# Queries scaled in their copies, negated row maxima, moved copies, and two more tiny matmuls at each feed-forward head

## The reference

```
h = h + 0.5 * swiglu(rms_norm(h), w_gate, w_up, w_down)      # four times, D_FF = 2816
s_own = einsum('bqhd,bkhd->bqhk', q, k); where(causal, s_own, -inf); softmax     # moba, q * 128**-0.5
logits = einsum('bqgrd,bkgd->bgrqk', q, k) * 64**-0.5; softmax                    # ab, heads 0 to 7
logits = einsum('bhqk'...) * 64**-0.5 + bias[rel]; softmax                        # ab, heads 8 to 15
logits = (q . k) * 96**-0.5; softmax                                              # mla, 16 heads
h = h + square(relu(rms_norm(h) @ w1)) @ w2                   # twice, D_FF_2 = 4096
```

## Time and profile before

| | |
|---|---|
| median of 3 runs | 1597.22 us (1592.72 to 1602.87) |
| profiled execution | 1598.15 us, span 1596.2 us |
| TensorE busy | 1527.6 us (96%) |
| DVE busy | 1020.2 us (64%) |
| ScalarE busy | 760.3 us (48%) |
| GpSimd busy | 413.0 us (26%) |
| mean granted TensorE clock | 0.982 of full speed |

### The profile page before, as it was taken

One profiled execution on the slowest core, in us unless ns is written; L12 is line 12 of the kernel. 1 busy time (PEld: TensorE's weight loads), 2 busy tenths in 40 slices (PEclk: granted clock), 3 DMA queues, 4 the chain that ended last, 5 costly groups with the idle time before them and its releaser, 6 DMA issues.

```text
span 1596.2 us, 31933 instructions
## 1 busy us (share of the span) xinstructions
PE 1527.6 (96%) x13406; PEld 1483.9 (93%) x13406; DVE 1020.2 (64%) x1010; ACT 760.3 (48%) x995; POOL 413.0 (26%) x376
## 2 busy tenths in 40 slices
PE   9999995999999999999799999989999988999997
PEld 7999985999999999999699999968999987799997
DVE  6777768575566655566576556566755576675555
ACT  6444542554445544366554444666434356543333
POOL 2999925010002000038320000773000033410000
PEclk9999996999999999999999999999999998999999
DMA  7555544445554555545245555442454541245552
GB/s 271 187 209 184 200 95 139 175 170 203 183 208 171 212 188 184 186 161 185 77 165 208 208 187 187 156 146 87 183 207 165 202 158 54 80 179 191 184 184 79
DMA packets 54822, 271.19 MB, mean 170 GB/s; under 512 B 17681, under 2 KB 22033, under 8 KB 23345
## 3 DMA queue, kind: packets, MB, share of 16 engines
q1 hardware_dynamic: 53648, 266.58, 46.8%
q0 software_dynamic: 1088, 3.38, 0.6%
HBM read 266.52 MB, written 3.42 MB: 169 GB/s over the span
## 4 chain that ended last, share of the span: by engine, by line
PE 80%; DVE 6%; POOL 4%; DMA 3%; ACT 3%; issue 2%; SPq 2%; DVEq 0%; POOLq 0%; ACTq 0%
PE ps L675 76%; DVE xlo L1658 2%; DVE wlo L1652 1%; DMA turned_y<-gs 1%; PE ps L1049 1%; POOL tsq L307 1%; DMA turned_u<-sq 1%; PE ps L1073 1%; PE ps L1061 1%; DVE h L1674 1%; ACT whi L1231 1%; DMA raw<-in_wstream 1%; ACT pm L1498 1%; SPq L417 1%; SPq L406 0%
## 5 line engine op out<-in xcount | busy, mean ns | idle before, releaser
L1652 DVE TENSOR_TENSOR wlo<-raw,whi 128x2048 fp32r<-128x2048 f32 x245 | 573.0, 2341 | 238.0 <-ACT whi L1231 237.8
L1231 ACT CAST whi<-raw 128x2048 fp32r<-128x2048 f32 x245 | 468.0, 1911 | 263.0 <-PE ps L675 250.2
L675 PE MATMUL ps<-xhi,whi 128*128 128x256 f32 x2048 | 574.8, 281 | 5.4 <-DVE xlo L1658 3.6
L675 PE MATMUL ps<-xlo,whi 128*128 128x256 f32 x2048 | 571.7, 279 | 0.0
L675 PE MATMUL ps<-xhi,wlo 128*128 128x256 f32 x2048 | 571.6, 279 | 0.0
L675 PEld LDWEIGHTS ps<-xhi,whi 128*128 128x128 f32 x2048 | 386.5, 189 | 9.3 <-DVE xlo L1658 3.2
L675 PEld LDWEIGHTS ps<-xhi,wlo 128*128 128x128 f32 x2048 | 389.6, 190 | 0.0
L675 PEld LDWEIGHTS ps<-xlo,whi 128*128 128x128 f32 x2048 | 386.2, 189 | 0.0
L675 PE MATMUL ps<-hhi,whi 128*128 128x256 f32 x1216 | 340.0, 280 | 1.9 <-DVE hlo L1732 1.9
L675 PE MATMUL ps<-hlo,whi 128*128 128x256 f32 x1216 | 339.9, 279 | 0.0
L675 PE MATMUL ps<-hhi,wlo 128*128 128x256 f32 x1216 | 339.8, 279 | 0.0
(11 more groups left out here) (259 smaller groups left out, 1887.8 us busy)
## 6 DMA issues: line engine op xcount, KB each, us to landing
raw<-in_wstream SPq DMA_DIRECT2D x245, 1024.0 KB, 4.8
raw<-in_wstream SPq DMA_DIRECT2D x4, 512.0 KB, 7.3
h<-in_xT SPq DMA_DIRECT2D x4, 256.0 KB, 5.5
turned_u<-sq SPq DMA_DIRECT2D x8, 128.0 KB, 4.3
uP<-turned_u SPq DMA_DIRECT2D x8, 128.0 KB, 2.9
turned_y<-gs SPq DMA_DIRECT2D x8, 128.0 KB, 2.5
sq<-turned_y SPq DMA_DIRECT2D x16, 64.0 KB, 2.3
biasA<-bias_rows POOLq DMA_DIRECT2D x5, 192.0 KB, 5.3
```

Of the source, the lines that this page charges most:

```text
L675: return pe.matmul(o, l, r, start=first, stop=last, skip_group_check=True)
L1231: act.copy(whi[:, slot, :], raw[:, slot, :]).then_inc(S("whi_ready"), 1)
L1652: dve.tensor_tensor(wlo[:, slot, :], raw[:, slot, :], whi[:, slot, :], ALU.subtract)\
```

## The change

Four edits. (1) The copies that bring the turned queries to `qT` multiply by the heads' scale; the scale disappears from the mask and bias additions, from the exponents and from the maxima. (2) The maximum is written negated straight to `nmx`, with no second instruction and no wait between; `mx` goes. (3) In ab the odd head's copy is made by DVE only where all heads 2p to 2p+5 have no bias, that is for pairs 0 and 1; pairs 2 and 3 move to ScalarE. mla has no bias and stays. (4) `proj` can put a `settle` between its two halves, on the half of the bank that is written next. In each ffn stage it does so in the head's second projection and in the second round's first; in each mlp stage in the second and third round's. ffn3's second `settle` goes.

```
-            def settle(bank):
-                mm(ps[0:32, bank, 0:64], zrow[0:1, 0:32], zrow[0:1, 0:64], True, True)
+            def settle(bank, c=0):
+                mm(ps[0:32, bank, c:c + 64], zrow[0:1, 0:32], zrow[0:1, 0:64], True, True)
...
                 for m in range(2 if stop_k is None else 1):
+                    if between and m == 1:
+                        settle(bank, T)
...
-                        proj(n, i, 4 + 2 * b, after_fp32=u == 0 and i is None)
+                        proj(n, i, 4 + 2 * b, after_fp32=u == 0 and i is None, between=u == 1 and i is None)
                         if u == 0 and i is None:
                             pe.wait_ge(S("root_ready"), roots_upto(k))
-                        proj(n + 1, i, 5 + 2 * b, after_fp32=st == "ffn3" and u == 0 and i is None)
+                        proj(n + 1, i, 5 + 2 * b, between=u == 0 and i is None)
...
-                        proj(n, i, 4 + (1 + u) % 3, after_fp32=u == 0 and i is None)
+                        proj(n, i, 4 + (1 + u) % 3, after_fp32=u == 0 and i is None, between=u > 0 and i is None)
...
+                        if kind == "q":
+                            turned_row = act.activation(dst, src, ACT.Copy, scale=HEADS[st][0]["scale"])
...
-                        act.activation(pm4[s % 4][:, t, :], src, ACT.Exp, scale=sc, bias=nmx[:, s % 4, t:t + 1],
+                        act.activation(pm4[s % 4][:, t, :], src, ACT.Exp, bias=nmx[:, s % 4, t:t + 1],
...
+        def odd_on_vector(hs, p):
+            return all(hd["bias"] is None for hd in hs[2 * p:2 * p + 6])
...
-                    if hs[2 * p + 1]["bias"] is not None:
+                    if not odd_on_vector(hs, p):
                         turned(2 * p + 1)
...
-                            dve.scalar_tensor_tensor(out=lg[b][:, t, 0:w], in0=ps[:, b, t * T:t * T + w],
-                                                     scalar=hd["scale"], in1=mask[:, t, 0:w], op0=ALU.mult, op1=ALU.add)\
+                            dve.tensor_tensor(lg[b][:, t, 0:w], ps[:, b, t * T:t * T + w], mask[:, t, 0:w], ALU.add)\
                                 .then_inc(S(st + "_lg"), 1)
...
-                            chain(dve.reduce_max(mx[:, b, t:t + 1], lg[b][:, t, 0:n_keys(hd, t)], AX.X))
-                        dve.tensor_scalar(nmx[:, b, :], mx[:, b, :], -1.0, None, ALU.mult).then_inc(S(st + "_nmx"), 1)
+                            reduced = dve.reduce_max(nmx[:, b, t:t + 1], lg[b][:, t, 0:n_keys(hd, t)], AX.X, negate=True)
+                        reduced.then_inc(S(st + "_nmx"), 1)
...
-                    chain(dve.reduce_max(mx[:, b, :], src, AX.X))
-                    dve.tensor_scalar(nmx[:, b, :], mx[:, b, :], -scale, None, ALU.mult).then_inc(S(st + "_nmx"), 1)
+                    dve.reduce_max(nmx[:, b, :], src, AX.X, negate=True).then_inc(S(st + "_nmx"), 1)
...
-                    if hs[2 * p + 1]["bias"] is None:
+                    if odd_on_vector(hs, p):
                         turned_odd(2 * p + 1)
```

More of the change, by code:

```diff
@@ L164, in build @@
         krp = sb("krp", [P, TT, 96])
-        mx = sb("mx", [P, 4, TT])
         nmx = sb("nmx", [P, 4, TT])
@@ L684, in chunk_ready, with proj @@
                 pe.wait_ge(S("wlo_ready"), at_iter(n + 1, BODY, i))
-            def settle(bank):
-                mm(ps[0:32, bank, 0:64], zrow[0:1, 0:32], zrow[0:1, 0:64], True, True)
-            def proj(n, i, bank, operand=None, wait_k=None, first_k=0, stop_k=None, after_fp32=False):
+            def settle(bank, c=0):
+                mm(ps[0:32, bank, c:c + 64], zrow[0:1, 0:32], zrow[0:1, 0:64], True, True)
+            def proj(n, i, bank, operand=None, wait_k=None, first_k=0, stop_k=None, after_fp32=False,
+                     between=False):
                 ohi, olo = operand or (xhi, xlo)
@@ L1428, in turned @@
                     if kind in "qk":
-                        dst = (qT if kind == "q" else kT)[:, i0:i0 + 2, :]
+                        dst, src = (qT if kind == "q" else kT)[:, i0:i0 + 2, :], bank2(bank)
                         if c["rev"]:
-                            act.copy(dst.rearrange("p m (t c) -> p (m t) c", t=TT), reversed_tiles(bank2(bank)))\
-                                .then_inc(S(st + "_rowT"), 1)
-                        else:
-                            act.copy(dst, bank2(bank)).then_inc(S(st + "_rowT"), 1)
+                            dst, src = dst.rearrange("p m (t c) -> p (m t) c", t=TT), reversed_tiles(src)
+                        if kind == "q":
+                            turned_row = act.activation(dst, src, ACT.Copy, scale=HEADS[st][0]["scale"])
+                        else:
+                            turned_row = act.copy(dst, src)
+                        turned_row.then_inc(S(st + "_rowT"), 1)
                     elif kind == "cq":
@@ L1494, in exponents @@
                         if hd["bias"] is None:
-                            src, sc = ps[:, SCORE_BANKS[s % 4], t * T:(t + 1) * T], hd["scale"]
+                            src = ps[:, SCORE_BANKS[s % 4], t * T:(t + 1) * T]
                         else:
-                            src, sc = lg[s % 2][:, t, :], 1.0
-                        act.activation(pm4[s % 4][:, t, :], src, ACT.Exp, scale=sc, bias=nmx[:, s % 4, t:t + 1],
+                            src = lg[s % 2][:, t, :]
+                        act.activation(pm4[s % 4][:, t, :], src, ACT.Exp, bias=nmx[:, s % 4, t:t + 1],
                                        accum_out=rs[:, s % 4, t:t + 1]).then_inc(S(st + "_exp"), 1)
@@ L1551, in turned_unit @@
                         act.wait_ge(S("mla_qt"), 2 * u + m + 1)
-                        act.copy(qT[0:96, 4 * u + 2 * m:4 * u + 2 * m + 2, :], bank2(4 + 2 * (u % 2) + m)[0:96])\
-                            .then_inc(S("mla_qTc"), 1)
+                        act.activation(qT[0:96, 4 * u + 2 * m:4 * u + 2 * m + 2, :], bank2(4 + 2 * (u % 2) + m)[0:96],
+                                       ACT.Copy, scale=HEADS["mla"][0]["scale"]).then_inc(S("mla_qTc"), 1)
                 queries(0)
@@ L1992, in maxima @@
                         dve.wait_ge(S(st + "_exp"), 2 * (s - 3))
-                    src, scale = bank2(bank), hd["scale"]
+                    src = bank2(bank)
                     if hd["bias"] is not None:
@@ L2001, in maxima @@
                         for t in range(TT):
-                            dve.scalar_tensor_tensor(out=lg[s % 2][:, t, :], in0=ps[:, bank, t * T:(t + 1) * T],
-                                                     scalar=scale, in1=row_[:, P - P * t:P - P * t + T],
-                                                     op0=ALU.mult, op1=ALU.add).then_inc(S(st + "_lg"), 1)
+                            dve.tensor_tensor(lg[s % 2][:, t, :], ps[:, bank, t * T:(t + 1) * T],
+                                              row_[:, P - P * t:P - P * t + T], ALU.add).then_inc(S(st + "_lg"), 1)
                         dve.wait_ge(S(st + "_lg"), 2 * hd["n_bias"] + 2)
-                        src, scale = lg[s % 2][:, :, :], 1.0
-                    chain(dve.reduce_max(mx[:, b, :], src, AX.X))
-                    dve.tensor_scalar(nmx[:, b, :], mx[:, b, :], -scale, None, ALU.mult).then_inc(S(st + "_nmx"), 1)
+                        src = lg[s % 2][:, :, :]
+                    dve.reduce_max(nmx[:, b, :], src, AX.X, negate=True).then_inc(S(st + "_nmx"), 1)
                 def turned_odd(s):
```

## The result

The changed kernel takes 1573.51 us (median of 4 runs, 1572.75 to 1575.22), the kernel before 1594.97 beside it (4 runs, 1592.22 to 1602.87): ratio 0.9859, 95% interval 0.9821 to 0.9897. That is 21.5 us less. The forecast was 1575 us, 22.4 less than the 1597.2 it started from.

A forecast was written before the change was run, and what follows sets the result against it. TensorE was taken as the bound, with 80% of the last-ending chain. From 1597.2 us, 14.7 (tiny matmuls, net) and 7.7 (attention) came off, giving 1574.8, forecast 1575 us; range 1566 to 1597.

The forecast's parts named there:

- What bounds the kernel: Whole kernel: 80% of the last-ending chain is TensorE; feed-forward streams keep 113.1 or 117.5 ns per matmul at clock 1.00.
- Cost of the tiny matmuls: Feed-forward heads: 11 more tiny matmuls at 0.33 us each, 3.6 us, nothing hiding it.
- Gain from the pace: ffn2, mlp0, mlp1: slow streams turn fast, 4.4 ns per following matmul, 18.3 us; 14.7 net.
- Two independent tries: Feed-forward heads: two tiny matmuls, from 3 fast of 6 outcomes, turn a slow stage fast with 0.75.
- Rival 1: Feed-forward streams: pace doesn't depend on the tiny matmuls, or slow stays slow; 1593.1 us; chance 0.23.
- Rival 2: Feed-forward streams: only one or two of the three slow stages convert; 1581 to 1587 us; chance 0.25.
- Rival 3: ffn0, ffn1, ffn3: new tiny matmuls turn fast streams slow, losing 18.7 us; 1612 us; chance 0.10.
- Attention: Attention stages: 7.7 us less on the path, moba 2.2, ab 3.7, mla 1.8; bounds zero and 12.
- Rival 4: Attention stages: folded negation was covered and gives nothing; 1583 us with the pace won; chance 0.07.
- The negation: Attention stages: folding it into the maximum, a reduce not held by GpSimd, removes 14.2 us of DVE time.
- The moved copies: ab, pairs 2 and 3: copies move from DVE to ScalarE, 0.6 us each there; part of ab's 3.7 us.
- Edits at nothing: Attention: scaled query copies at most 0.5 us, mostly hidden; mask and bias additions without multiply, and dropping mx, nothing.

The follow-up runs named there:

- e7: Changed kernel with a tiny matmul between the halves of all 20 gate and up projections of ffn1's loop, 18 more; 1580.37 us, ratio 0.9922.
- e1: Kernel before with only edit (4), the tiny matmuls, and no attention edits; 1582.78 us, ratio 0.9923.
- e11: e3 without the tiny matmul at each head behind the fp32 sums; 1592.65 us, ratio 0.9997 to the kernel before.
- e10: e9 with one more tiny matmul in the second chunk of the out-projections of ab and mla; 1578.34 us, ratio 0.9916 to the kernel before.
- e8: Changed kernel with the between-halves tiny matmul in fp32r, with values of xhi, instead of bf16 zeros; 1604.74 us, ratio 1.0064 to the kernel before.
- e2: Changed kernel with edit (4) taken back, attention edits kept; 1587.29 us, ratio 0.9944 to the kernel before.
- e6: Changed kernel with the odd copies of pairs 2 and 3 in ab back on DVE; 1574.40 us, ratio 0.9884 to the kernel before.
- e9: e3 with one more tiny matmul in ffn0, behind the wait at about 49 us; 1575.31 us, ratio 0.9897 to the kernel before.
- e12: Changed kernel with the two in-stream tiny matmuls of each head in fp32, not zeros, instead of bf16; 1586.22 us, ratio 0.9972 to the kernel before.
- e3: Changed kernel without the second new tiny matmul of each head, the first kept; 1572.74 us, ratio 0.9856 to the kernel before.
- e5: Changed kernel with a separate negation again, done as a second maximum over one element; 1575.49 us, ratio 0.9890 to the kernel before.
- e4: Changed kernel with the separate negation back as a multiply by -1 after the maximum; 1581.00 us, ratio 0.9914 to the kernel before.

## Why the prediction was right, step by step

**What bounds the kernel** held. TensorE's streams set the time, at two paces with the clock granted in full, and the pace stays from one restart to the next.

**Cost of the tiny matmuls**: 0.33 us each, forecast. e7 measured 0.35. ffn1, fast in both profiles, grew by 0.7 us for its two. ffn3 grew by 0.6 for one net: its first 9 us, up to the first new tiny matmul, ran slow this time, which is the other 0.3.

**Gain from the pace**: forecast 18.3 us gross, 14.7 net. The profile shows 16.2 from the three slow stages, their own cost taken off, and 1.3 lost in ffn1 and ffn3, so 14.9, with ffn0 left out as in the forecast. The ratio of e1 gives 12.3 (8.3 to 16.1). 14.7 lies within that interval, so the sum isn't refuted, but that it met the profile this closely has luck in it. A forecast from one profile takes its draw for the kernel's typical one, and that draw had ffn2 slow, which it was in 5 of 13 profiles. By the heads counted above, the two squared-relu stages were slow whenever nothing had been put ahead of them (2 x 1368 x 4.4 ns = 12.0 us), ffn2 5 times of 13 (2.4 us on the mean) and ffn1 2 of 13 (1.0); less 3.8 for eleven tiny matmuls at 0.35 this estimate gives 11.6 us, near e1's 12.3. So most of the gain is two stages that were always slow, and the smaller part is a draw. The draw is also part of the spread: one stage is worth about 6 us (1416 x 4.4 ns).

**"Two independent tries" was wrong**, though the value that I took (slow always turns fast, at the first of the two) came true. The outcome isn't a coin. A bf16 tiny matmul in a fast stream left it fast, 86 times of 86. In a slow stream begun by another one in the usual way it made it fast, 25 of 25. In any other slow stream it left it slow, 9 of 9. So the head's tiny matmul, which was there already, prepares the turn and the first new one completes it; alone, neither is enough (the head's gave 41 fast and 37 slow in these profiles, and e11, with the in-stream one alone, was no faster than the kernel before). The 0.75 had no ground, and that the first of the two always converts was a choice of one end of a bound: that it came true was luck, since nothing in the forecast's reasons distinguished a head that prepares the turn from one that doesn't. What the second new one is for is seen only indirectly: e10's ffn2 had an unusual head, one wasn't enough, and it left the pattern from which a further one has always worked. No run had a second one in that place, so that it would rescue the stage is argued, not shown. Nearest to it are mlp0 and mlp1 of e10, where the second one was the head's and the fp32 sums lay between; both turned fast.

**Rival 1** (slow stays slow, 1593 us) didn't happen in the changed kernel; slow does stay slow where no tiny matmul had begun the stream in the usual way (e10, and e11 with 1592.65 us). **Rival 2** (some convert) didn't happen. **Rival 3** (fast turned slow) is what the same matmul does in fp32r (e8: 1604.74 us with the attention edits in it; the rival said 1612). bf16, fp32r and fp32 did three different things, which no step of the prediction had considered; the values differed too (zeros only in bf16), and no run separates the two. A stream of one shape at one clock had two paces here, 113.3 and 117.8 ns. The isolated gap that the Trainium skill gives in "TensorE: Matmul & The Clock Gate", section "Back-to-back issue gap", 109 ns at 256 columns, is met by neither.

**Attention**: forecast 7.7 us; e2 gives 8.9 (5.1 to 12.9), and the changed kernel against e1 9.3 by medians. Rival 4 (nothing) fell. By stage, from the start of the first score matmul to that of the last value matmul, the profiles must be set side by side at the same granted clock, which differs from one to the next (us; a stage with matmul records missing is left out):

```
      clock      without the edits   with them                        forecast
moba  1.00       24.4 (before)       22.7, 22.8 (e6, e7, e11)         -2.2
ab    1.00       37.4 (e1)           33.0, 33.1 (e2, e9)              -3.7
ab    0.95       37.4 (before)       33.0, 33.8 (e10, e12)            -3.7
ab    0.90                           34.4 to 34.8 (after, e3, e7)
mla   0.95-0.96  38.6 (e1)           37.2 to 38.0 (after, e3, e7,     -1.8
                                     e9, e11)
mla   0.84       42.1 (before)
```

So the edits gave 1.7 us in moba, 3.6 to 4.4 in ab and 0.6 to 1.4 in mla, 5.9 to 7.5 together. All three forecasts have the right size, ab's the best. Before against after, read without the clock, would have said 0.8, 3.0 and 4.1; but of mla's 4.1 us 3.5 are there without the attention edits too (e1, at a clock of 0.96 instead of 0.84). Each value without the edits is that of one profile. The forecast had named a lower clock in ab as a sign of being wrong, and it did fall, from 0.95 to 0.90 over the stage, but that took at most 1.4 us (34.4 against the 33.0 at 1.00) from a larger gain. Why the clock of these stages differs between kernels that are the same there isn't settled.

**The negation** was the right piece. That a reduction wouldn't be held rested on a page; e5 shows it, with 157 ns as the longest. The rule in the Trainium skill's "SBUF — State Buffer", section "Who interferes with whom" agrees with both groups, 1009 ns and 157 ns. The negation alone comes to 7.5 us by e4's median, as much as the 7.7 that was forecast for all of attention, and that is more than its stages show: at like clock e4 is 1.3 to 1.6 us longer in moba (24.9), 1.5 to 2.3 in ab (35.3) and 0.4 in mla (39.0), some 3 to 4 together. Its profiled execution was the fastest of its six, 3.7 us under the median, so where the rest lies isn't known.

**The moved copies** were to give part of ab's 3.7. In the kernel's time they gave nothing that shows (e6); in ab, at like clock, 0.8 to 1.5 us may be theirs. The three stops of TensorE in ab went because the maxima ahead of the copies had lost their held negations: in e6, where the copies are back on DVE, 0.19 us of waiting is left. GpSimd's waits for exponents in moba barely changed (20.2 us in total before, 19.4 after).

**Edits at nothing**: nothing in the profile speaks against it; no run had the scaled copies or the plain additions alone, so it isn't shown.

## What to carry to other kernels

When two stretches of the same instructions run at different paces and the granted clock is equal, count instructions per microsecond from restart to restart, in several executions and stage by stage: here two stages were always slow and one was slow now and then, and one profile alone can't tell these apart. A matmul of the same size in another type (and with other values) had the opposite effect; try the cheap variants rather than reason by size. Set attention stages side by side only at the same granted clock. And a small VectorE multiply beside GpSimd work may take six times its own time (1009 against 169 ns): where a reduction can write the final form, let it. Here that removed forty of them, 14.3 us of VectorE time, and 3 to 8 us of the kernel.

## What the runs showed of the hardware that was not expected

- A stream of 256-column fp32r matmuls with 128x128 weights has two steady paces at granted clock 1.00, 113.3 and 117.8 ns, and keeps either for a stage of 1500.
- One matmul of 1x32 weights and 64 columns, 0.35 us of stream, can set it: bf16 left fast streams fast (86 of 86) and turned slow ones fast where another one had begun them (25 of 25); fp32r turned fast streams slow and left slow ones slow, and the kernel ended at 1604.74 us; fp32 swapped the pace each time (1586.22 us).
- The patterns behind the restart differ by a few nanoseconds (226 114 118 against 222 117 118), yet tell whether the next one will turn the stream. Why there are two paces at all stays open, as does e9's missing gain: ffn0's pace is set again at a wait at 49 us (fast in eight of the profiles, the changed kernel's among them, slow in e2, e5, e6, e7, e8 and e10), and this is likely the largest part of the spread that is left: from ffn0's norm sums to those of the next stage it is 185.8 to 187.9 us where fast and 189.0 to 191.4 where slow. No run shows how to fix it there.
